# Queueing seven small-constant loads later in the weight stream of a two-layer backbone kernel

## Chip, cores and metric

One Trainium2 chip, one core of it. The metric is the device time of one execution in microseconds (us); for a program on one core that is the time of this core. Several executions are summed up by their median.

## What is computed

The reference is a two-layer block of a flow-matching generator over 512 latent tokens and 256 context tokens of width 1024, in float32. What matters here is its beginning. A conditioning vector for the latent tokens and one for the context tokens go through SiLU and are multiplied by a 1024 x 6144 matrix per layer; that gives six modulation vectors per stream (shift, scale and gate of two sub-layers):

```
s_lat = silu(c);  s_ctx = silu(c_ctx)[None]
mod_l = split((s_lat @ ada_w[layer] + ada_b[layer])[:, None, :], 6)
mod_c = split((s_ctx @ ada_w[layer] + ada_b[layer])[:, None, :], 6)
a_lat = rms_norm(h, ln1_g) * (1 + mod_l[1]) + mod_l[0]
a_ctx = rms_norm(hc, ln1_g) * (1 + mod_c[1]) + mod_c[0]
```

Layer 0 then multiplies both by a combined input projection (the columns of a gated DeltaNet part and of a grouped-query attention part), and uses some small constants: two vectors of 16 (`dt_bias`, `a_log`) for the gates, norm gains of 64 for the output, the queries and the keys (`go`, `gq`, `gk`), a table of cosines and sines for the rotary embedding (`rope`), short convolution weights (`cw`) and two triangular masks for the cumulated gates. After the mixer comes a routed mixture of 16 experts; layer 1 is a neighbourhood attention and again a mixture of experts, and a final norm ends it.

## The kernel before, in words

All large weights pass through a ring of eight slots of 512 KB in SBUF (`RING = 8`). A list named `stream` fixes their order: first the 32 modulation units of layer 0 (kind "ada", units 0 to 31: rows of 128 of `ada_w`, 1024 columns each, for shift and scale), then twelve units of the input projection (kind "blk": four `wrest` of 288 KB, four `wq` and four `wz` of 512 KB), then modulation units 32 to 47 of layer 0 (the gates), all 48 modulation units of layer 1, the convolution part of the projection, and so on. The function `stream_units` (L2286 and on) walks this list on the SP engine. Before unit u it waits until unit u - 8 has been used (`w_free`), and then issues the one DMA of the unit (L2294 for "ada", L2312 for "blk").

Ahead of the stream SP issues five loads (L2322 to L2326): identity and ones (`base`), the conditioning vectors (`cT`), the norm gains (`lnT`), the selection matrix (`sel`) and the modulation bias (`adab`). Behind the fifth modulation unit, inside `stream_units`, it issues the tokens: `ctx` (1 MB, L2296) and `x` (2 MB, L2297) into the tile H. Right behind these come the small constants of later stages: `masks` (L2299), `dt_bias`, `a_log` and `go` (one loop, L2302), `gq` (L2303), `gk` (L2305), `rope` (L2307) and `cw` (L2308). These eight loads write 128, 8, 8, 32, 256, 64, 128 and 18 KB, 642 KB or 0.65 MB together. Seven of these are counted by one semaphore, `masks` by its own. `dt_bias`, `a_log`, `go`, `gq` and `gk` are read with a stride of zero over the 128 partitions; `gq` is also repeated eight times and `gk` twice within a partition, so that these two are written in runs of 64 values (256 bytes), 1024 runs and 256 runs. SP issues in program order, so every later unit stands behind them.

TensorE takes the 32 modulation units one by one (`ada_matmuls`, its matmuls at L241), each as soon as it has landed, and each frees its slot. Then VectorE adds the bias (L274), TensorE transposes the vectors into columns (L249), VectorE copies and combines them (L284, L291) and normalises the six token tiles (L342), TensorE transposes these (`norm_pe`, L366) while VectorE and ScalarE apply scale and shift (L353, L330), and TensorE begins the input projection (`proj_pe`, L458), whose first group of eight matmuls needs all four `wrest` units. ScalarE squares the tokens for their norm (L318) when `ctx` and `x` have landed.

The first users of the small constants: VectorE at L498 (in `gates_dve`, which waits for all seven with `qtp_load` before it), TensorE at L536 for the masks (in `gates_pe`), and after these the head norms with their gains and the rotary table, the convolution and the output norm.

Of the kernel before, what the change touches and what calls it, by code (L numbers as in the profile page):

```python
# [141 lines left out]
def build(nc, t, out):  # L142

    ctx = ExitStack()
    with ctx:
# [81 lines left out]
        def ada_unit(l, n):  # L227

            r, k, i = n // 16, n % 16 // 2, n // 16 + 3 * (n % 2)
            return t["ada_w"][l, k * P:(k + 1) * P, i * D:(i + 1) * D], r, k, i  # L230
# [2055 lines left out]
        def stream_units(sp, lo, hi):  # L2286
            for u in range(lo, hi):
                kind, args = stream[u]
                if u >= RING:
                    sp.wait_ge(w_free, u - RING + 1)  # L2290
                slot, sig = ring[:, u % RING, :], w_land[u % RING]
                if kind == "ada":
                    l, n = args
                    sp.dma_start(slot, ada_unit(l, n)[0]).then_inc(sig, 16)  # L2294
                    if (l, n) == (0, 4):
                        sp.dma_start(H[:, 0:CT, :], t["ctx"].rearrange("(t p) d -> p t d", p=P)).then_inc(x_in, 16)  # L2296
                        sp.dma_start(H[:, CT:NT, :], t["x"].rearrange("(t p) d -> p t d", p=P)).then_inc(x_in, 16)  # L2297
                    if (l, n) == (0, 4):
                        sp.dma_start(MSUM, t["masks"].rearrange("p (d n) -> p d n", d=2)) \  # L2299
                            .then_inc(masks0_in, 16)  # L2300
                        for dst, name in ((DTB, "dt_bias"), (ALOG, "a_log"), (GO, "go")):
                            sp.dma_start(dst, t[name].partition_broadcast(P)).then_inc(qtp_load, 16)  # L2302
                        sp.dma_start(GAIN[:, 0:512].rearrange("p (h d) -> p h d", d=HD),  # L2303
                                     t["gq"].partition_broadcast(P).unsqueeze(1).broadcast_to([P, 8, HD])).then_inc(qtp_load, 16)
                        sp.dma_start(GAIN[:, 512:640].rearrange("p (h d) -> p h d", d=HD),  # L2305
                                     t["gk"].partition_broadcast(P).unsqueeze(1).broadcast_to([P, 2, HD])).then_inc(qtp_load, 16)
                        sp.dma_start(ROPE, t["rope"].rearrange("p (t w c) -> p t w c", t=LT, w=2)).then_inc(qtp_load, 16)  # L2307
                        sp.dma_start(CW, t["cw"].rearrange("p (c w) -> p c w", w=3)).then_inc(qtp_load, 16)  # L2308
                elif kind == "blk":
                    b, k2 = args  # L2310
                    N = 2 * WIDTH[b]
                    sp.dma_start(slot[:, 0:N], t[("wrest", "wq", "wz")[b]][k2]).then_inc(sig, 16)  # L2312
                elif kind == "conv":
                    sp.dma_start(slot, t["wconv"][args[0]]).then_inc(sig, 16)
                elif kind in ("wout0", "wout1", "wv"):
                    sp.dma_start(slot, t[kind][args[0] * P:(args[0] + 1) * P, :]).then_inc(sig, 16)
                else:
                    sp.dma_start(slot, t[kind][args[0]]).then_inc(sig, 16)

        @block.sync  # L2320
        def _(sp):
            sp.dma_start(base_t[:, :], t["base"]).then_inc(consts_in, 16)  # L2322
            sp.dma_start(cT, t["cT"]).then_inc(small_in, 16)
            sp.dma_start(lnT_t[:, :], t["lnT"]).then_inc(small_in, 16)
            sp.dma_start(SEL, t["sel"].rearrange("p (s m) -> p s m", s=8)).then_inc(consts_in, 16)
            sp.dma_start(rows_t[:, :], t["adab"][0]).then_inc(rows_in, 16)  # L2326
            stream_units(sp, 0, U_OUT0)
            dn_sync(sp)
            stream_units(sp, U_OUT0, U_MOE[0])
            rows_sync(sp, 0)  # L2330
            moe_sync(sp, 0)
            sp.wait_ge(mp["x_free"], 24 * NPAIR)
            stream_units(sp, U_MOE[0], len(stream))
            rows_sync(sp, 1)
            moe_sync(sp, 1)
            for i in range(LT):
                sp.wait_ge(end_ok, i + 1)
                sp.dma_start(out[i * P:(i + 1) * P, :], FIN[:, i, :]).then_inc(all_out, 16)
            sp.wait_ge(all_out, 16 * LT)
# [136 lines left out]
```

## Time and profile before

| | |
|---|---|
| median of 3 runs | 2627.17 us (2625.91 to 2636.28) |
| the profiled execution, own time | 2635.99 us |
| its span in the trace | 2634.2 us |
| mean granted TensorE clock | 0.914 of full |
| TensorE matmul busy | 2160.6 us (82%) |
| VectorE, ScalarE, GpSimd busy | 697.3, 462.5, 171.6 us |
| chain that ended last | PE 63%, DMA 22%, DVE 10%, ACT 2% |

The page cuts the span into 40 equal slices of 65.9 us. The row of PE gives its busy share in tenths, PEclk the granted clock in tenths, DMA the mean busy share of the 16 DMA engines; here the first slices matter, of which the first has PE at 4, DMA at 8 and the second PE at 8, DMA at 2. The chain of work that ended last is followed back from the last instruction: what stands in it set the end of the program, and what does not stand in it was covered by something else. In the trace an issue (SPq) is the time that SP's queue spends on a DMA instruction; when the data has landed is told separately, as a time from the issue on.

### The profile page before, as it was taken

The page shows a single profiled execution, that of the slowest core. Times are in us where ns is not written, and L with a number is a line of the kernel's source. Part 1 is how long each engine was busy: PE and PEld are TensorE (multiplying, and loading weights), DVE is VectorE, ACT ScalarE, POOL GpSimd, SP SyncE. Part 2 cuts the span into 40 slices and gives each one's busy share as a digit, 9 for nine tenths or more (in the row PEclk, how much of TensorE's full clock was granted, in tenths as well). Part 3 has the DMA queues.
Part 4 walks back from the last instruction along what each step waited for, and adds up shares of the span by engine and source line. Part 5 has one row for each costly group of instructions (what it writes and reads, how often), then busy time and mean ns, then how long its engine had stood idle before and what let it go on. Part 6 is the DMA issues. An engine that isn't in the chain of part 4 may idle for free.

```text
span 2634.2 us, 31425 instructions
## 1 busy us (share of the span) xinstructions
PE 2160.6 (82%) x13016; PEld 1117.4 (42%) x13016; DVE 697.3 (26%) x1289; ACT 462.5 (18%) x1025; POOL 171.6 (7%) x156
## 2 busy tenths in 40 slices
PE   4897999963786957999999977999999487777774
PEld 0543566643686433333333323554895222222221
DVE  0205332259867251001111112000553500000001
ACT  1014322166520011000000002000551100000001
POOL 0000000011111000111111010000000000000000
PEclk8898999985757988999999988999999699999997
DMA  8215532014112337999999971111212399999996
GB/s 308 109 41 206 159 120 81 15 34 129 65 34 97 136 137 265 369 388 385 394 393 393 399 265 40 56 32 62 83 49 89 128 387 413 415 414 415 414 415 236
DMA packets 113955, 564.30 MB, mean 214 GB/s; under 512 B 13552, under 2 KB 26352, under 8 KB 64672
## 3 DMA queue, kind: packets, MB, share of 16 engines
q1 hardware_dynamic: 102080, 522.55, 50.9%
q0 software_dynamic: 10416, 34.58, 4.8%
q10 hardware_dynamic: 1328, 5.24, 0.6%
q8 instruction: 104, 1.70, 0.3%
q14 instruction: 27, 0.22, 0.0%
HBM read 532.87 MB, written 29.46 MB: 213 GB/s over the span
## 4 chain that ended last, share of the span: by engine, by line
PE 63%; DMA 22%; DVE 10%; ACT 2%; issue 2%; SPq 1%; POOL 0%; DVEq 0%; ACTq 0%; POOLq 0%
PE ps L1805 14%; DMA work_sb<-expert_w_up 8%; PE ps L1569 5%; PE ps L1813 5%; DMA work_sb<-expert_w_gate 5%; DMA work_sb<-expert_w_down 5%; PE ps L458 4%; PE ps L2071 4%; PE ps L754 3%; PE ps L643 2%; PE ps L2049 2%; PE ps L2058 2%; PE ps L241 2%; PE ps L2134 2%; DMA ring_sb<-ada_w 2%
## 5 line engine op out<-in xcount | busy, mean ns | idle before, releaser
L1805 PE MATMUL ps<-work_sb 128*32 128x512 f32 (+1 forms) x2304 | 364.9, 600 | 75.3 <-DMA work_sb<-expert_w_gate 32.3
L1805 PE MATMUL ps<-ring_sb,work_sb 128*32 128x512 f32 (+1 forms) x2304 | 362.6, 601 | 64.2 <-DMA ring_sb<-expert_w_up 27.9
L1805 PEld LDWEIGHTS ps<-work_sb 128*32 128x32 f32 (+1 forms) x2304 | 114.3, 120 | 308.4 <-issue 308.0
L1805 PEld LDWEIGHTS ps<-ring_sb,work_sb 128*32 128x32 f32 (+1 forms) x2304 | 108.6, 120 | 290.2 <-issue 272.3
L1913 DVE TENSOR_TENSOR work_sb<-ps,work_sb 128x512 f32<-128x512 f32 x32 | 20.6, 686 | 658.5 <-PE ps L1813 330.4
L1569 PE MATMUL ps<-ring_sb,work_sb 128*128 128x512 f32 x320 | 139.6, 599 | 2.7 <-DVE work_sb L2199 1.9
L241 PE MATMUL ps<-ring_sb,sT_sb 128*32 128x512 f32 x384 | 99.3, 674 | 42.1 <-DMA ring_sb<-ada_w 42.1
L1884 ACT ACTIVATE work_sb<-ps 128x1024 f32<-128x1024 f32 x16 | 16.4, 1024 | 606.9 <-PE ps L1805 306.5
L1964 POOL DMA_INDIRECT hl_rows<-work_sb x32 | 45.6, 1426 | 966.1 <-DVE work_sb L1927 868.3
L458 PE MATMUL ps<-ring_sb,work_sb 128*128 128x512 f32 (+1 forms) x288 | 105.9, 530 | 0.9 <-DVE work_sb L353 0.9
L1813 PE MATMUL ps<-ring_sb,work_sb 128*32 128x512 f32 x768 | 101.1, 596 | 0.0
L1813 PE MATMUL ps<-work_sb 128*32 128x512 f32 x768 | 100.7, 592 | 0.0
L754 PE MATMUL ps<-work_sb,ring_sb 128*128 128x512 f32 x192 | 98.0, 592 | 0.0
L2071 PE MATMUL ps<-ring_sb,work_sb 128*128 128x512 f32 x224 | 96.3, 592 | 0.0
L1569 PEld LDWEIGHTS ps<-ring_sb,work_sb 128*128 128x128 f32 x320 | 61.2, 192 | 79.8 <-issue 76.2
L1927 DVE SCALAR_TENSOR_TENSOR work_sb<-ps,work_sb,gates_sb 128x1024 f32<-128x1024 f32 x16 | 20.6, 1284 | 281.5 <-PE ps L1813 149.8
L1889 ACT COPY work_sb<-ps 128x512 f32<-128x512 f32 x32 | 17.9, 588 | 349.2 <-PE ps L1852 349.1
L458 PEld LDWEIGHTS ps<-ring_sb,work_sb 128*128 128x128 f32 x288 | 54.6, 190 | 51.6 <-issue 45.4
L643 PEld LDWEIGHTS ps<-work_sb 128*128 128x128 f32 x448 | 53.5, 191 | 39.4 <-issue 38.6
L2058 PE MATMUL ps<-work_sb,ring_sb 128*128 128x512 f32 x128 | 65.3, 592 | 0.0
L2071 PEld LDWEIGHTS ps<-ring_sb,work_sb 128*128 128x128 f32 x224 | 42.6, 190 | 53.6 <-issue 53.6
L695 DVE TENSOR_REDUCE work_sb<-ps 128x1 f32<-128x768 f32 (+1 forms) x48 | 37.4, 780 | 102.9 <-PE ps L633 80.9
(363 smaller groups left out, 2805.5 us busy)
## 6 DMA issues: line engine op xcount, KB each, us to landing
work_sb<-expert_w_gate SPq DMA_DIRECT2D x64, 1024.0 KB, 9.6
ring_sb<-expert_w_gate SPq DMA_DIRECT2D x64, 1024.0 KB, 13.3
ring_sb<-expert_w_up SPq DMA_DIRECT2D x64, 1024.0 KB, 16.2
work_sb<-expert_w_up SPq DMA_DIRECT2D x64, 1024.0 KB, 14.0
ring_sb<-expert_w_down SPq DMA_DIRECT2D x64, 1024.0 KB, 15.4
work_sb<-expert_w_down SPq DMA_DIRECT2D x64, 1024.0 KB, 12.9
ring_sb<-ada_w SPq DMA_DIRECT2D x96, 512.0 KB, 5.0
ring_sb<-wout SPq DMA_DIRECT2D x16, 512.0 KB, 6.4
```

The source lines that it names most:

```text
L241: mm = pe.matmul(ps[32 * q:32 * q + 32, bank, :], sT[:, k, :], w[:, a * 512:(a + 1) * 512], start=(k == 0), stop=(k == KT - 1))
L458: mm = pe.matmul(ps[:, j % 4, 0:N], A[:, k, tok_cols(tt):tok_cols(tt) + P], w[:, (k % 2) * N:(k % 2 + 1) * N], start=(k == 0), stop=(k == ...
L643: mm = pe.matmul(ps[:, 6, n % 8 * HD:(n % 8 + 1) * HD], PT[:, n % 2, c * P:(c + 1) * P], VB[:, c, kv * HD:(kv + 1) * HD], start=(c == 0), ...
L754: mm = pe.matmul(ps[:, b, :], w[:, k, :], A[:, k, LO:LO + LAT], start=(k == 0), stop=(k == KT - 1))
L1569: mm = pe.matmul(ps[:, 4 + j % 4, :], c(k), w[:, half * 512:half * 512 + 512], start=(k == 0), stop=(k == KT - 1))
L1805: mm = pe.matmul(ps[g:g + wide, bank + n, :], lat_src[:, k, g:g + wide], us[e][:, n * 512:(n + 1) * 512], start=(k == 0), stop=(k == KT - 1))
L1813: mm = pe.matmul(ps[g:g + 32, bank_c, :], ctx_src(k, e), us[e][:, n * 512:(n + 1) * 512], start=(k == 0), stop=(k == KT - 1))
L1964: pool.indirect_dma_start(hl_rows, at(TOKH[0:CAP_L, 2 * p + e:2 * p + e + 1]), YL0[r], None, compute_op=ALU.add) \
L2049: mm = pe.matmul(ps[:, c % 4, :], w[:, k, :], AO[:, k, LO:LO + LAT], start=(k == 0), stop=(k == KT - 1))
L2058: mm = pe.matmul(ps[:, b, :], w[:, k, :], AO[:, k, LO:LO + LAT], start=(k == 0), stop=(k == KT - 1))
L2071: mm = pe.matmul(ps[:, 2 * (m % 2) + half, :], AO[:, k, v_cols(m):v_cols(m) + P], w[:, half * 512:half * 512 + 512], start=(k == 0), stop= ...
L2134: mm = pe.matmul(ps[:, 5 + g % 2, n % 8 * HD:(n % 8 + 1) * HD], OPT[:, n % 2, c * P:(c + 1) * P], VO[:, m, h * HD:(h + 1) * HD], start=(c ...
```

## The change

The condition under which the small constants are issued names modulation unit 31 in place of unit 4. The two token loads, `ctx` and `x`, stay behind unit 4. Nothing else differs: the same eight loads, in the same order, with the same semaphores, now behind the 32nd unit and ahead of the first `wrest` unit.

```diff
@@ -2295,7 +2295,7 @@
                     if (l, n) == (0, 4):
                         sp.dma_start(H[:, 0:CT, :], t["ctx"].rearrange("(t p) d -> p t d", p=P)).then_inc(x_in, 16)
                         sp.dma_start(H[:, CT:NT, :], t["x"].rearrange("(t p) d -> p t d", p=P)).then_inc(x_in, 16)
-                    if (l, n) == (0, 4):
+                    if (l, n) == (0, 31):
                         sp.dma_start(MSUM, t["masks"].rearrange("p (d n) -> p d n", d=2)) \
                             .then_inc(masks0_in, 16)
                         for dst, name in ((DTB, "dt_bias"), (ALOG, "a_log"), (GO, "go")):
```

## Rows read from the trace of the kernel before

**Rows 1.** The chain that ended last, 0 to 260 us: start us, us, what.

```profile
12.91 6.80 SPq L2305
...
22.38 17.18 DMA ring_sb<-ada_w
39.60 4.50 PE ps L241 x12
...
93.30 105.96 PE ps L458 x288
```

**Rows 2.** Six stretches: us, PE, PEld, DVE, ACT, POOL busy, PEclk, DMA share, GB/s.

```profile
15.70:22.00 6.30, 0.04 (x2) 0.00 (x0) 0.00 (x0) 0.00 (x0) 0.00 (x0) 0.85 1.03 401
22.00:32.00 10.00, 0.00 (x0) 0.00 (x0) 0.00 (x0) 7.92 (x14) 0.00 (x0) 0.50 0.09 23
32.00:39.60 7.60, 0.00 (x1) 0.00 (x1) 0.00 (x0) 0.00 (x0) 0.00 (x0) 0.50 0.66 249
39.60:74.20 34.60, 28.86 (x104) 4.05 (x104) 0.69 (x1) 0.00 (x0) 0.00 (x0) 0.89 1.01 396
...
93.30:199.00 105.70, 105.70 (x288) 54.63 (x288) 3.77 (x19) 7.78 (x12) 5.22 (x1) 1.00 0.15 49
```

**Rows 3.** Timeline of SP's DMA issues, 0 to 260 us: start us, us, engine line.

```profile
6.80 2.10 SPq L2299 DMA_DIRECT2D work_sb<-masks  x1
...
12.43 0.44 SPq L2303 DMA_DIRECT2D work_sb<-gq  x1
...
21.90 0.43 SPq L2308 DMA_DIRECT2D work_sb<-cw  x1
22.38 41.63 SPq L2294 DMA_DIRECT2D ring_sb<-ada_w  x27
64.95 6.54 SPq L2312 DMA_DIRECT2D ring_sb<-wrest  x4
```

**Rows 4.** DMA packets of the stretch 24 to 28 us.

```profile
DMA packets 256, 0.07 MB, mean 16 GB/s; under 512 B 256, under 2 KB 256, under 8 KB 256
```

**Rows 5.** DMA issues, 0 to 260 us: KB each, median us from issue to landing.

```profile
ring_sb<-wrest SPq DMA_DIRECT2D x4, 288.0 KB, 7.9
...
work_sb<-gq SPq DMA_DIRECT2D x1, 256.0 KB, 21.7
...
work_sb<-gk SPq DMA_DIRECT2D x1, 64.0 KB, 22.7
...
work_sb<-cw SPq DMA_DIRECT2D x1, 18.0 KB, 16.5
```

**Rows 6.** Timeline of all engines, 0 to 130 us: start us, us, engine line.

```profile
14.69 1.05 PE L241 MATMUL ps<-ring_sb,sT_sb 128*32 128x512 f32 x4 [0.23 <-DMA ring_sb<-ada_w]
...
22.32 1.06 ACT L318 ACTIVATE work_sb<-h_sb 128x1024 f32<-128x1024 f32 x1 [18.51 <-DMA h_sb<-x]
...
39.60 6.14 PE L241 MATMUL ps<-ring_sb,sT_sb 128*32 128x512 f32 x20 [23.86 <-DMA ring_sb<-ada_w]
...
61.30 1.05 PE L241 MATMUL ps<-ring_sb,sT_sb 128*32 128x512 f32 x4 [0.22 <-DMA ring_sb<-ada_w]
...
62.58 1.05 PE L241 MATMUL ps<-ring_sb,sT_sb 128*32 128x512 f32 x4 [0.23 <-DMA ring_sb<-ada_w]
...
66.64 1.05 PE L241 MATMUL ps<-ring_sb,sT_sb 128*32 128x512 f32 x4 [1.73 <-DMA ring_sb<-ada_w]
...
74.22 1.05 PE L241 MATMUL ps<-ring_sb,sT_sb 128*32 128x512 f32 x4 [0.20 <-DMA ring_sb<-ada_w]
...
97.48 0.29 DVE L484 COPY work_sb<-ps 128x128 f32<-128x128 f32 x1 [4.24 <-PE ps L458]
...
117.50 0.26 DVE L498 TENSOR_TENSOR work_sb<-work_sb 128x96 f32<-128x96 f32 x1
```

**Rows 7.** Matmuls with the masks (L536): count, duration ns, first and last start us.

```profile
L536 PE MATMUL ps<-work_sb x24: 269/361/363, 204.2 to 211.1; 128*128 128x8 f32 x24
```

**Rows 8.** SP's waits over the whole span: us in total, times, longest us.

```profile
SPq L1979 <- PE ps L1813: 475.7, 92, 57.9
```

## The prediction
> **What bounds the kernel now.** I read the chain that ended last first, and in it only the start, since the change touches nothing behind the input projection by itself. There the chain goes through SP's issue of `gk`, then through the wait of modulation unit 5 for its data, then through the modulation matmuls, and at 93.30 us it enters 106 us of gap-free projection matmuls [rows 1]. So the time to the first L458 matmul lies on the path in full. The timeline tells how it is spent [rows 6]: units 0 to 4 are used by 15.74 us; unit 5 starts at 39.60, after 23.86 us without a matmul; then a unit starts every 1.28 us (61.30, 62.58), with one hiccup ahead of 66.64; the last, unit 31, starts at 74.22; 19.08 us later the projection starts.
>
> Next the stretches [rows 2]. Up to 22.0 us the 16 DMA engines are full (share 1.03, 401 GB/s): that part of the hole is `ctx` and `x`, and ScalarE gets `x` at 22.32 [rows 6]. From 22 to 32 us the share is 0.09 at 23 GB/s, and the stretch 24 to 28 us moves 256 packets, all below 512 bytes [rows 4]: 64 a us. That is the pattern of `gq`'s 1024 runs of 256 bytes, issued at 12.43 [rows 3] and landed 21.7 us later [rows 5], at 34.1. `gk` lands at 12.91 + 22.7 = 35.6 and `cw` at 21.90 + 16.5 = 38.4, and unit 5, issued at 22.38, starts at 39.60, right behind them. So the queue is worked off in order, and small runs hold up the large load behind them. During the modulation stream itself the bound is the DMA (396 GB/s; a unit is 1.05 us of matmul in a beat of 1.28).
>
> **The change part by part.**
>
> Removed from behind unit 4: eight loads, 0.65 MB, and 22.33 - 6.80 = 15.5 us of SP's issue time [rows 3]. Units 5 to 7 then follow `x` at 6.75 us. The DMA engines are full until 22.0 and would simply go on: unit 5 is there one beat after `x`, at 22.32 + 1.28 = 23.6, against 39.60. That is 16.0 us. Some bytes of the constants moved before 22 us beside `x`: of the 0.65 MB, 0.23 moved from 22 to 32 us (10 us at 23 GB/s) and the 0.15 of `rope` and `cw` later, which leaves 0.27 MB, 0.7 us at 401 GB/s. The gain is between 16.0 and 16.7 us; I take 16.5, unit 5 at 23.1.
>
> Kept: the beat. 26 units from 39.60 to 74.22 take 34.62 us, hiccup and all. TensorE's clock was at 0.50 in the rows from 22 us on [rows 2], the lower level of 1.2 GHz, and even so the first five units took 6.14 us [rows 6], 1.23 each, below the beat. The idle time left, 15.7 to 23.1 us, still lets the clock fall (0.85 as the mean of 15.7 to 22.0), so those first units run slow again, hidden behind the DMA. I cost the clock at nothing; with the cover gone it would be (1.23 - 1.05) x 5 = 0.9 us. Unit 31 starts at 74.22 - 16.5 = 57.7 us, and the projection is ready for its weights at 93.30 - 16.5 = 76.8.
>
> Added behind unit 31: the same eight loads, ahead of `wrest`, `wq` and `wz`. Two resources are passed. (a) SP's queue: unit 31 waits for unit 23's slot, so SP issues it at about 64.0 - 16.5 = 47.5, the constants follow until 47.5 + 15.5 = 63.0 at the old pace, and `wrest` 0 goes out at 63.0. It went out at 64.95 before [rows 3], with 28.35 us in hand against 93.30 and 7.9 us needed [rows 5]: that slack of 20 us pays for the move. (b) The DMA queue: before, a large load became usable 39.60 - 22.32 = 17.3 us after the last large one ahead of the constants. Put behind unit 31 this gives 57.7 + 17.3 = 75.0 for `wrest` 0, against a need at 76.8: cover 1.8 us. The other three are smaller than a modulation unit (288 against 512 KB, 0.7 us a piece) and the eight matmuls of the first group last 4.24 us [rows 6], so they keep ahead. The lower bound: with fewer runs outstanding than at 12.43 us, `gq` may be worked on from its issue, 47.5 + 5.6 = 53.1; its visible work of 34.1 - 22.3 = 11.8 us and the remaining 39.60 - 34.1 = 5.5 us then end at 70.4. The upper bound: unit 5's full 17.2 us from issue to use, counted from 63.0, is 80.2, which is 3.4 us late. I take 75.0, since it measures the queue from the last large landing, which is how the rows line up; so nothing is lost, and both ends are kept for the range. A late `wrest` would delay TensorE one for one; `wq`, issued next, has 23 us more.
>
> Users of the constants: they have landed by about 75 us. The first user, L498, would run at 117.50 - 16.5 = 101.0 [rows 6], and the masks are first read at 204.2 - 16.5 = 187.7 [rows 7]. Cover 26 us and more: no cost. No wait is added on any engine, and `qtp_load`, on which VectorE and ScalarE wait, is complete long before.
>
> Behind 93.30: TensorE is busy for all of 105.70 us at full clock [rows 2]. Further on SP's issues wait for slots that matmuls free, the largest such wait being 475.7 us in the expert stage [rows 8]; SP thus cannot run ahead on its own, and all that follows should move as a block.
>
> Sum: 16.5 us gained, nothing given back. On the profiled execution: 2635.99 - 16.5 = 2619.5 us. That execution is 8.8 us above the median of 2627.17, so the same difference there gives **2610.7 us**, 0.63% less.
>
> A page weighed against the rows: the stretch 22 to 32 us shows small runs at 23 GB/s. The Trainium skill, DMA: Bandwidth & Descriptors, section "Anatomy of one DMA", fits a transfer as 2.0 us plus its bytes at 436 GB/s (measured for loads issued from GpSimd). By that fit the constants' 0.65 MB would occupy the engines for 1.5 us, and the sum would be about 1.5 us instead of 16.5. The trace disagrees with it for this queue. The same page, section "Bandwidth", says that transfers under 64 KB are descriptor-dominated; with that the rows agree.
>
> **The rivals.**
>
> *Late weights.* The hole moves from unit 5 to the first `wrest` instead of vanishing. For it: the cover is only 1.8 us, and by issue time it is -3.4. Against it: fewer loads are outstanding when `gq` is issued, 4.6 us of stream (57.7 - 53.1) against 9.9 (22.3 - 12.4). Price: up to 3.4 us, plus perhaps 1 us for a TensorE whose clock is lower; the gain is then 12.1 to 16, at worst 2627.17 - 12.1 = 2615.1 us.
>
> *Slower than before.* The constants are worked off one load at a time: place, the DMA queue between unit 31 and `wrest`. If `gk` began only when `gq` had landed, both with their full times, then 53.1 + 21.7 + 22.7 + (39.60 - 35.6) = 101.5, 24.7 us past the need of 76.8; less the 16.5 gained that is 8.2 us slower, 2635.4, and over 0.5% slower from 29.6 us of lateness on. It decides from a landing of `wrest` 0 after 93.3. Against it: before, `gk` landed 1.5 us after `gq`, and 64 packets a us would have to become half as many.
>
> *The bytes alone matter.* The hole from 22 to 39 us isn't the constants' but follows on any load behind `x`; removing them gives their 0.65 MB, 0.65 / 0.401 = 1.6 us, and the time is 2625.6. Against it: that stretch holds nothing but small packets. The Trainium skill's fit, quoted above, would come out there too.
>
> That the change does not do what it says is hardly possible: unit (0, 31) is in the list once, and ahead of `wrest`.
>
> **How the numbers follow.** A measurement of this kernel can tell about 0.5% (13.1 us) from no change; the three runs shown already spread by 10.4 us. Forecast 0.76, late weights 0.16, bytes alone 0.05, slower 0.03. The forecast's 16.5 clears the 13.1 by 3.4 us, and scatter of medians eats that in about 1 of 6 cases: 0.64 faster, 0.12 same. Late weights: 0.07 faster, 0.09 same. Bytes alone: same. The slow rival: 0.02 slower, 0.01 same. Together 0.71, 0.27, 0.02. The range takes the gain from 12.1 to 16.7 and about 4 us of scatter on either side, rounded: 2606 to 2619, with a little more on the low side since the highest of the three runs shows that the scatter of before is not centred: 2605 to 2619.
>
> **What would show each step.** Right: no idle time of TensorE over 9 us before 60 us; unit 5 at 22.5 to 24 us; DMA share near 1 up to 57 us, and only then a stretch of about 0.06 to 0.1; unit 31's matmul at 57 to 58.5; first L458 at 76 to 78 with VectorE as its releaser. Wrong: that matmul released by the DMA of `wrest`, a first L458 past 80, a hole left at unit 5, or a projection longer than 106 us. If all these fit and the time is still not 16 us lower, something behind 93 us did not move with the block, and the forecast is wrong there.

## The result, and the profile after

Twenty runs of the changed kernel have a median of 2617.38 us (2609.35 to 2627.28), twenty of the kernel before 2628.98 us (2623.09 to 2636.42). The ratio is 0.995 with a 95% interval of 0.9941 to 0.9959: 0.5% faster, about 13.1 us, between 10.8 and 15.5. (The two medians alone differ by 11.6 us, 0.44%.) The profiled execution took 2622.86 us with a span of 2621.1 us (mean granted clock 0.917). The forecast was 2610.7 us, 0.63% less; the time lies inside the range of 2605 to 2619, and the gain is 3 to 5 us smaller than the 16.5 forecast.

The chain that ended last, first 260 us of the changed kernel, answers to [rows 1] (start us, us, what). SP's issues of `gk` have left it, the wait of unit 5 ends at 23.3 instead of 39.6, and the projection enters at 77.07 instead of 93.30 with the same 105.96 us of work:

```profile
6.62 16.68 DMA ring_sb<-ada_w
23.35 4.52 PE ps L241 x12
...
77.07 105.96 PE ps L458 x288
```

The timeline of all engines, which answers to [rows 6]:

```profile
22.04 1.06 ACT L318 ACTIVATE work_sb<-h_sb 128x1024 f32<-128x1024 f32 x1 [17.86 <-DMA h_sb<-x]
...
23.35 6.19 PE L241 MATMUL ps<-ring_sb,sT_sb 128*32 128x512 f32 x20 [7.95 <-DMA ring_sb<-ada_w]
...
50.28 1.05 PE L241 MATMUL ps<-ring_sb,sT_sb 128*32 128x512 f32 x4 [1.55 <-DMA ring_sb<-ada_w]
...
57.96 1.05 PE L241 MATMUL ps<-ring_sb,sT_sb 128*32 128x512 f32 x4 [0.22 <-DMA ring_sb<-ada_w]
...
77.07 53.16 PE L458 MATMUL ps<-ring_sb,work_sb 128*128 128x288 f32 x165 [0.91 <-DVE work_sb L353]
...
101.27 0.26 DVE L498 TENSOR_TENSOR work_sb<-work_sb 128x96 f32<-128x96 f32 x1
```

Unit 5 starts one beat after `x`; TensorE's idle time before it fell from 23.86 to 7.95 us. The hiccup in the stream is there again (1.55 us, at 50.28). The first projection matmul is still released by VectorE, not by a DMA, so the weights were there.

SP's issues, which answer to [rows 3], and below them the time to landing of `gq` and `gk`, which answers to [rows 5]:

```profile
6.62 41.21 SPq L2294 DMA_DIRECT2D ring_sb<-ada_w  x27
47.87 1.00 SPq L2299 DMA_DIRECT2D work_sb<-masks  x1
...
50.33 0.43 SPq L2303 DMA_DIRECT2D work_sb<-gq  x1
50.81 4.36 SPq L2305 DMA_DIRECT2D work_sb<-gk  x1
...
58.35 10.01 SPq L2312 DMA_DIRECT2D ring_sb<-wrest  x4
```

```profile
work_sb<-gq SPq DMA_DIRECT2D x1, 256.0 KB, 16.2
...
work_sb<-gk SPq DMA_DIRECT2D x1, 64.0 KB, 17.7
```

The slow stretch of the DMA has moved, it has not vanished. Stretches of the changed kernel (columns as in [rows 2]):

```profile
23.00:58.00 35.00, 29.00 (x106) 4.05 (x108) 0.69 (x1) 6.97 (x14) 0.00 (x0) 0.88 0.99 390
...
58.00:60.00 2.00, 1.12 (x5) 0.24 (x6) 0.69 (x1) 0.00 (x0) 0.00 (x0) 1.00 0.07 18
60.00:62.00 2.00, 1.10 (x8) 0.90 (x8) 0.87 (x13) 0.00 (x0) 0.00 (x0) 1.00 0.07 20
...
68.00:70.00 2.00, 2.00 (x11) 1.90 (x10) 0.92 (x2) 0.67 (x2) 0.00 (x0) 0.50 0.68 174
70.00:72.00 2.00, 2.00 (x12) 1.97 (x10) 1.51 (x2) 1.02 (x2) 0.00 (x0) 0.50 0.99 320
```

It now lies under the bias add, the transposes and the normalisation, which wait for no weights, and is over by 70 us, before the projection asks for them.

### The profile page after: what moved, and what is told of

The parts are those of the page before. It is cut to its first block, busy times and chain, and to the rows that moved or that the text cites. A ratio compares the mean times of both kernels' runs of the same rounds, so it can differ in the third digit from the quotient of the medians.

```text
span 2621.1 us, 31425 instructions
## 1 busy us (share of the span) xinstructions
PE 2159.6 (82%) x13016; PEld 1113.8 (42%) x13016; DVE 698.7 (27%) x1289; ACT 462.1 (18%) x1025; POOL 169.9 (6%) x156
## 4 chain that ended last, share of the span: by engine, by line
PE 63%; DMA 22%; DVE 9%; ACT 2%; issue 2%; SPq 1%; POOL 0%; DVEq 0%; ACTq 0%; POOLq 0%
PE ps L1805 14%; DMA work_sb<-expert_w_up 7%; PE ps L1569 5%; PE ps L1813 5%; DMA work_sb<-expert_w_gate 5%; DMA work_sb<-expert_w_down 5%; PE ps L458 4%; PE ps L2071 4%; PE ps L754 3%; PE ps L643 2%; PE ps L2049 2%; PE ps L2058 2%; PE ps L241 2%; PE ps L2134 2%; DMA ring_sb<-expert_w_up 2%
## 5 line engine op out<-in xcount | busy, mean ns | idle before, releaser
L1805 PE MATMUL ps<-work_sb 128*32 128x512 f32 (+1 forms) x2304 | 364.9, 600 | 74.2 <-DMA work_sb<-expert_w_gate 32.7
L1805 PE MATMUL ps<-ring_sb,work_sb 128*32 128x512 f32 (+1 forms) x2304 | 365.0, 605 | 66.5 <-DMA ring_sb<-expert_w_up 31.0
L1805 PEld LDWEIGHTS ps<-work_sb 128*32 128x32 f32 (+1 forms) x2304 | 114.5, 120 | 306.9 <-issue 306.5
L1805 PEld LDWEIGHTS ps<-ring_sb,work_sb 128*32 128x32 f32 (+1 forms) x2304 | 109.4, 121 | 293.7 <-issue 275.9
L1569 PE MATMUL ps<-ring_sb,work_sb 128*128 128x512 f32 x320 | 139.6, 599 | 2.7 <-DVE work_sb L2199 1.9
L458 PE MATMUL ps<-ring_sb,work_sb 128*128 128x512 f32 (+1 forms) x288 | 105.9, 530 | 0.9 <-DVE work_sb L353 0.9
L1813 PE MATMUL ps<-ring_sb,work_sb 128*32 128x512 f32 x768 | 101.4, 598 | 0.0
L1813 PE MATMUL ps<-work_sb 128*32 128x512 f32 x768 | 100.7, 592 | 0.0
L1927 DVE SCALAR_TENSOR_TENSOR work_sb<-ps,work_sb,gates_sb 128x1024 f32<-128x1024 f32 x16 | 20.5, 1284 | 280.5 <-PE ps L1813 149.8
L1569 PEld LDWEIGHTS ps<-ring_sb,work_sb 128*128 128x128 f32 x320 | 61.2, 192 | 79.8 <-issue 76.2
L458 PEld LDWEIGHTS ps<-ring_sb,work_sb 128*128 128x128 f32 x288 | 54.6, 190 | 51.6 <-issue 45.4
## 6 DMA issues: line engine op xcount, KB each, us to landing
ring_sb<-expert_w_down SPq DMA_DIRECT2D x64, 1024.0 KB, 13.6
work_sb<-expert_w_down SPq DMA_DIRECT2D x64, 1024.0 KB, 12.7
```

The lines of the kernel that those rows point to most:

```text
L458: mm = pe.matmul(ps[:, j % 4, 0:N], A[:, k, tok_cols(tt):tok_cols(tt) + P], w[:, (k % 2) * N:(k % 2 + 1) * N], start=(k == 0), stop=(k == ...
L1569: mm = pe.matmul(ps[:, 4 + j % 4, :], c(k), w[:, half * 512:half * 512 + 512], start=(k == 0), stop=(k == KT - 1))
L1805: mm = pe.matmul(ps[g:g + wide, bank + n, :], lat_src[:, k, g:g + wide], us[e][:, n * 512:(n + 1) * 512], start=(k == 0), stop=(k == KT - 1))
L1813: mm = pe.matmul(ps[g:g + 32, bank_c, :], ctx_src(k, e), us[e][:, n * 512:(n + 1) * 512], start=(k == 0), stop=(k == KT - 1))
```

## The experiments

Twelve runs were made, eight of variants and four of unaltered copies. The comparisons with the kernel before use its runs on the same chip. A ratio is the time over that of the kernel before, with its 95% interval. "L458" below is the start of the first projection matmul, 93.30 us in the profile of before and 77.07 in that of the changed kernel.

### Which load makes the hole: e1 and e2

The first moves `gq` alone behind unit 31, the second moves the other seven and leaves `gq`. The edit of e1, shortened:

```diff
-                        sp.dma_start(GAIN[:, 0:512]..., t["gq"]...)          # at (0, 4)
...
+                    if (l, n) == (0, 31):
+                        sp.dma_start(GAIN[:, 0:512]..., t["gq"]...)
```

> Only the load of gq (1024 runs of 256 bytes) is moved behind unit 31; the other seven constants stay behind unit 4. Theory 'runs' (the hole is made by the number of small runs, most of them gq's): gq's visible 11.8 us go, unit 5 starts at about 27.8 us instead of 39.60, and the first L458 matmul at about 81.5. Rival 'any load behind x' (the small loads hold up the stream by being there, not by their runs): seven of eight loads remain, so unit 5 stays past 36 us and L458 past 90.

> gq alone stays behind unit 4, the other seven constants go behind unit 31. Theory 'runs': gq keeps its 11.8 us and only the rest of the hole goes; unit 5 at about 35 us, first L458 at about 89. Rival 'any load behind x': one of eight loads remains, unit 5 at 25 us or earlier, L458 at 79.

With `gq` alone late, unit 5 starts at 29.58 us and L458 at 82.70, a gain of 10.6 us in the profile; the ratio is 0.9963 (0.9949 to 0.9978). With `gq` alone left, unit 5 starts at 35.13 and L458 at 88.57, a gain of 4.7; the ratio is 0.9983 (0.9964 to 1.0001). Both are within 2 us of what was expected for `gq` as the main part, and unit 5 is over 6 us from where "any load behind x" wanted it. The two parts add up to 15.3 of the 16.2 us.

### Number of runs or their source: e3, e4 and e8

e3 keeps the order and lays the repeats into the row, so that `gq` is 128 runs of 2 KB (and `gk` 128 runs of 512 bytes). e4 keeps `gq`'s 1024 runs of 256 bytes, but gives each an address of its own. The edit of e4, shortened:

```diff
-        gq=c(a["even_q_norm_g"][0]),
+        gq=c(np.tile(a["even_q_norm_g"][0], (P, 8, 2))),
...
-                                     t["gq"].partition_broadcast(P).unsqueeze(1).broadcast_to([P, 8, HD]))
+                                     t["gq"][:, :, 0:HD])
```

> All eight constants stay behind unit 4, but gq and gk come from inputs laid out with the repeats inside the row, so that gq is 128 runs of 2 KB and gk 128 runs of 512 bytes: the same 320 KB are written, in 256 runs instead of 1280. Theory 'runs': 1024 runs fewer, unit 5 at 26 to 29 us, first L458 at 80 to 83. Rival 'bytes alone': the same bytes, so unit 5 stays at 39.6 and L458 at 93.3.

> All constants stay behind unit 4; gq is again written in 1024 runs of 256 bytes, but every run is read from an address of its own, 512 bytes from the next, instead of all from the same 256 bytes. Theory 'runs': nothing changes, unit 5 at 38.5 to 40.5 us. Rival 'one source' (reading the same 256 bytes 1024 times is what is slow): the hole shrinks as with wide rows, unit 5 at 26 to 29 us.

e3: unit 5 at 28.35 us, L458 at 82.11, ratio 0.9966 (0.9948 to 0.9985). So the bytes are not it. But e3 alone can't tell the number of runs from the number of reads of one address, since it lowers both.

e4 can, and it refutes the reading that I had put on record, that small runs as such are slow: with as many runs of the same size, unit 5 starts at 28.36 us and L458 at 81.23; ratio 0.9957 (0.9935 to 0.9979). `gq` lands 11.4 us after its issue at 12.58, at 24.0, instead of at 34.1. The timeline of TensorE in e4:

```profile
28.36 4.91 PE L241 MATMUL ps<-ring_sb,sT_sb 128*32 128x512 f32 x16 [12.49 <-DMA ring_sb<-ada_w]
```

DMA packets of e4 in the stretch 20 to 24 us, and of the kernel before in the same stretch:

```profile
DMA packets 2089, 1.14 MB, mean 285 GB/s; under 512 B 1748, under 2 KB 1949, under 8 KB 2089
```

```profile
DMA packets 1036, 0.83 MB, mean 207 GB/s; under 512 B 769, under 2 KB 897, under 8 KB 1036
```

1748 small packets in 4 us are 437 a us, those of all loads together; before, 769 passed in the same stretch (192 a us), and behind it 64 a us [rows 4]. So what makes the greater part of the hole is that the 1024 reads go to the same 256 bytes. Why such reads are slow no run shows, and no distance but 512 bytes was tried.

e8 reads all five broadcast constants from addresses of their own, again with the order of before:

> The kernel before with its order (all constants behind unit 4), but all five broadcast constants (dt_bias, a_log, go, gq, gk) read every run from an address of its own, in the same number of runs. Theory 'one source': what is left of the hole is the bytes and a little for the number of runs, so unit 5 starts at 25 to 27 us (28.36 with gq alone apart) and the first L458 at 78 to 80, nearly what the move gives. Rival 'runs': unit 5 stays at 28 us or later, because the number of runs is as before.

Its unit 5 starts at 26.59 us, inside the 25 to 27 expected, and L458 at 80.28, 0.3 us past the 80; ratio 0.9953 (0.9937 to 0.9968). All eight constants stay ahead of unit 5 and the hole is nearly gone. What is left against the changed kernel, 26.59 - 23.35 = 3.2 us, is by my estimate 1.6 us of bytes (0.65 MB at 401 GB/s) and 1.6 us that I leave to the number of runs without having tested it.

### A queue of their own: f2

The kernel before, with the eight loads issued by ScalarE's queue at about 4 us (`act.dma_start` behind the first activation), so that the stream isn't behind them.

> The kernel before, but the eight constants are issued by ScalarE, right after its first activation (about 4 us), so that they have a queue of their own and the weight stream doesn't stand behind them. Theory 'one queue' (the slow reads of one row hold up only what is queued behind them on the same queue): the DMA engines stay full, unit 5 starts at 24 to 26 us, first L458 at 77.5 to 79.5. Rival 'the engines are held' (the slow reads keep the DMA engines themselves from other work): a hole of some 10 us stays wherever they run, unit 5 or a later unit is late, and L458 starts past 85.

Unit 5 starts at 35.12 us and L458 at 89.51; ratio 0.9993 (0.9974 to 1.0011). The theory "one queue" falls. The first L458 comes 3.8 us earlier than before, not 16, and the ratio can't be told from no change. The stream is not queued behind the constants and is held up all the same: `x` lands later (ScalarE's first square at 31.12 instead of 22.32). Stretches of that kernel (columns as in [rows 2]):

```profile
18.00:22.00 4.00, 0.00 (x0) 0.00 (x0) 0.00 (x0) 0.00 (x0) 0.00 (x0) 0.72 0.79 213
22.00:26.00 4.00, 0.00 (x0) 0.00 (x0) 0.00 (x0) 0.00 (x0) 0.00 (x0) 0.50 0.85 233
26.00:30.00 4.00, 0.00 (x0) 0.00 (x0) 0.00 (x0) 0.00 (x0) 0.00 (x0) 0.50 0.64 209
34.00:38.00 4.00, 2.88 (x8) 0.38 (x8) 0.00 (x0) 3.98 (x9) 0.00 (x0) 0.50 1.00 383
```

From 22 to 26 us 211 small packets pass, 53 a us, much as in [rows 4]; large packets pass beside them, and all together the engines move little more than half of what they moved before. The packets of that stretch by queue, SP's (q1) and ScalarE's (q10), with MB and share of the engines:

```profile
q1 hardware_dynamic: 214, 0.88, 79.4%
q10 hardware_dynamic: 211, 0.05, 5.7%
```

The two queues get as many packets through as each other, here and in every stretch of 2 us from 12 to 34 us (192 and 190 from 12 to 14, 98 and 98 from 30 to 32). So the engines work the two queues packet for packet, and the large loads are held to the pace of the slow reads. The Trainium skill, DMA: Bandwidth & Descriptors, section "Issuing engines are not separate DMA queues", says that DMAs of all issuing engines run on the same 16 engines and interleave; this run agrees. Where such loads stand in time counts for more than which queue they are on.

### How much cover the move has: e7

The changed kernel, with `gq` issued twice behind unit 31, the second time into a free area (`SQJ`), and the two waits for the constants raised from seven loads to eight.

> The changed kernel with the load of gq issued twice behind unit 31, the second time into a scratch area that is free then. It measures the cover of the first wrest unit. A second gq costs the DMA queue 1024 reads of one 256-byte row, at the 64 a us of the trace 16 us. If the cover is the 1.8 us of the prediction, the first L458 matmul waits for the DMA of wrest and starts at about 77.1 + 14.2 = 91.3; if it is 5 us, as the changed kernel's DMA share suggests (near 1 from 70 us on), at 88; if the weights were there much earlier (10 us or more), at 83 or before.

The timeline of that kernel around its first projection matmul:

```profile
76.89 5.22 POOL L2445 MEMSET work_sb<- 128x6144 f32 x1 [75.83 <-DVE work_sb L353]
86.57 1.46 PEld L458 LDWEIGHTS ps<-ring_sb,work_sb 128*128 128x128 f32 x4 [10.78 <-issue]
86.60 1.78 PE L458 MATMUL ps<-ring_sb,work_sb 128*128 128x288 f32 x3 [10.62 <-DMA ring_sb<-wrest]
```

GpSimd's memset starts when the activations are complete, at 76.89; TensorE starts 9.7 us later, when `wrest` lands. That is between the 83 and the 88 expected, nearest to a cover of 5 us. The rival "late weights" is real as a mechanism. TensorE waits one for one, and after this idle time it starts at the lower clock (0.53 as the mean of 86.6 to 92 us), so that the projection itself takes 108.43 instead of 105.95 us: 2.5 us more, where the prediction had put "perhaps 1 us". `gk` lands at 55.63 + 27.7 = 83.3 us instead of 50.81 + 17.7 = 68.5, so the second `gq` cost the queue 14.8 us. By this estimate `wrest` would have been usable without it at 86.60 - 14.8 = 71.8 us, and the cover in the changed kernel is 77.07 - 71.8 = 5.3 us.

### Something else to move: f1

The changed kernel, and `sel` (512 KB) goes behind unit 31 as well, its wait with it.

> The changed kernel, and the selection matrix sel (512 KB, first read by the gate matmuls past 200 us) goes with the constants behind unit 31 too, ahead of them. If the stretch up to unit 31 is bound by the bytes ahead of it, 0.52 MB at 410 GB/s are 1.3 us: first L458 at 75.8 instead of 77.07, still released by VectorE. Rival 'the cover is used up': wrest now stands behind 0.52 MB more and the first L458 waits for its DMA, at 77 or later.

Half a miss. L458 starts at 76.78 us, released by VectorE, so the cover held; but of the 1.3 us expected only 0.3 came, and unit 5 did not come earlier at all (23.58). Its DMA moved 335 GB/s from 4 to 8 us and 368 from 8 to 12, against 387 and 402 in the changed kernel: what was taken out ahead was given back by a slower start, which I can't explain. The ratio is 0.9944 (0.9923 to 0.9966); no difference to the changed kernel (0.995) can be told from that, and no other variant has a lower ratio than the changed kernel.

### Where the rest of the gain went: e5, e6, f3 and f4

Unaltered copies, to see what one profile is worth.

> The changed kernel once more, unaltered, for a second profile of it. Theory 'scatter' (the 3 us by which the gain at the end of the profiles falls short of the 16.2 us at the projection come from stretches that last differently from one execution to the next: the gate matmuls at L259, the DeltaNet stage, the expert stage of layer 0): the first L458 again at 77 us within 0.5, but at least one of these three stretches differs from the first profile by over 2 us. Rival 'given back by the change': all three stretches last as in the first profile within 1 us.

> The kernel before once more, unaltered, for a second profile. Theory 'scatter': the first L458 at 93.3 us within 0.5, and at least one of the three stretches (L259 to L599, L993 to L1569, L1805 to the last L1813) differs from the first profile of before by over 2 us. Rival 'given back by the change': they repeat within 1 us.

> The changed kernel for a third profile. From the start of L259 to the start of L599 its first two profiles took 14.6 and 13.8 us, against 11.0 and 12.4 in the two of before. Theory 'the clock at L259 depends on where the work falls': 13.5 us or more again. Rival 'chance': anything from 11 to 14.6.

> The kernel before for a third profile, to go with the third of the changed one. Theory 'the clock at L259 depends on where the work falls': at most 12.8 us from L259 to L599 again, and the first L458 at 92.5 to 93.5. Rival 'chance': anything from 11 to 14.6.

Durations of stages in us, and in the first row the start of the first L458; three executions each (before; e6; f4 and after; e5; f3):

| | before | after |
|---|---|---|
| first L458 | 93.3, 92.6, 92.2 | 77.1, 77.0, 76.9 |
| L458 to first L599 | 147.3, 148.4, 147.5 | 150.9, 150.3, 150.7 |
| of it L259 to L599 | 11.0, 12.8, 11.1 | 14.6, 13.8, 16.2 |
| L599 to DeltaNet (L993) | 329.1, 329.1, 329.0 | 329.0, 329.0, 330.7 |
| L993 to L1569 | 293.6, 291.5, 287.2 | 291.6, 287.4, 288.3 |
| experts of layer 0 (L1805 to last L1813) | 544.6, 544.5, 545.5 | 548.3, 544.1, 544.8 |

The first L458 of e6 (92.64) and of f4 (92.23) lie 0.2 and 0.3 us below the ranges expected for them, and the "12.4" in the expectation of f3 is 12.8 in the trace. Two things come out. First, scatter: the DeltaNet stage lasts 287.2 to 293.6 us whichever kernel it is, and the experts 544.1 to 548.3; a single pair of profiles can show from 7.9 us (f4 and after) to 20.5 us of gain (before and e5) at the end of the span. The first theory, that all of the shortfall is of this kind, is not enough, though: the stretch from L458 to L599 does not scatter much and is longer in the changed kernel, 150.6 against 147.8 on average, 2.9 us. It is the gate matmuls (L259). Of the kernel before, then of the changed one, from the timeline of TensorE:

```profile
229.59 1.96 PE L259 MATMUL ps<-modrows_sb,work_sb 128*128 128x512 f32 x4 [1.89 <-DVE modrows_sb L274]
232.65 1.99 PE L259 MATMUL ps<-modrows_sb,work_sb 128*128 128x512 f32 x4 [1.10 <-ACT gates_sb L267]
```

```profile
213.35 3.75 PE L259 MATMUL ps<-modrows_sb,work_sb 128*128 128x512 f32 x4 [2.19 <-DVE modrows_sb L274]
218.21 3.78 PE L259 MATMUL ps<-modrows_sb,work_sb 128*128 128x512 f32 x4 [1.10 <-ACT gates_sb L267]
```

The same four matmuls take 3.75 instead of 1.96 us, twice over. The granted clock says why; two stretches of the kernel before, up to L259 and from there on, then the same two of the changed kernel:

```profile
211.80:227.80 16.00, 12.46 (x55) 2.60 (x55) 13.29 (x22) 6.37 (x11) 0.00 (x0) 0.71 0.66 233
228.00:240.00 12.00, 7.10 (x15) 2.71 (x16) 11.73 (x23) 3.04 (x3) 0.00 (x0) 0.98 0.52 209
```

```profile
195.50:211.50 16.00, 12.45 (x55) 2.64 (x55) 13.23 (x22) 6.36 (x11) 0.00 (x0) 0.71 0.64 232
211.80:221.80 10.00, 7.35 (x8) 2.35 (x8) 9.79 (x20) 1.01 (x1) 0.00 (x0) 0.50 0.61 248
```

In both kernels the clock falls to its lower level (0.50, 1.2 GHz) after TensorE has waited for the last modulation units (2.27 us before, 2.01 after); read in rows of 1 us it stays there for some 3 us in this profile of before, and for some 13 us in that of after, through the first two groups. A slow group by itself is no mark of the changed kernel: in e6, an unaltered copy of before, the first group took 3.75 us too, and in e8 3.36. In the profiles of after, e5 and f3 two or three groups were slow. The stretch from L458 to L599 separates most of the variants: 147.3 to 148.4 us in before, e6, f4, e2, e3, e4, e8 and f2; 150.1 to 151.0 in after, e5, f3, f1 and e1. The second list is kernels that load `gq` behind unit 31, but not all of them. e7 loads it there as well; of its 150.9 us, 2.5 are the slower start of its projection, and the 148.5 that are left put it beside the first list, with a single slow group (3.64 us). From L259 to L599 it is 13.6 to 16.2 us in the second list against 11.0 to 12.8 in the first and 12.7 in e7. I have no cause for it: in the two profiles shown the waits of TensorE ahead of L259 differ by 0.3 us (1.89 and 2.19) and the mean clock of the 16 us before it is the same, 0.71. "The clock at L259 depends on where the work falls" held in its numbers; but e1 runs L259 at 219.0 us and is slow, e3 runs it at 218.5 and is fast, so the place in time alone is not it. That the 2.9 us come from the change, and not from the executions that happened to be profiled, is likely by these counts and not shown.

With it the account closes as far as the scatter lets one see. The starts of L458 differ by 92.7 - 77.0 = 15.7 us on average; less 2.9 us given back at L259 that is 12.8 us, inside the interval of 10.8 to 15.5. The spans of the same six profiles differ by 15.3 us on average, since the later stages together were 2.5 us shorter in the three of after, which is less than the DeltaNet stage alone scatters.

## Why the prediction was right, and what of it was wrong

- **The hole before unit 5.** Forecast 23.1 us between 22.9 and 23.6; measured 23.35. The DMA engines simply went on behind `x`. Right, and the two bounds held it.
- **The beat and the hiccup.** 26 units in 34.62 us; measured 57.96 - 23.35 = 34.61. Unit 31 at 57.7 against 57.96. The clock was indeed down for the first of them (6.19 us for five units) and the DMA hid it.
- **SP's queue.** Constants at 47.5 against 47.87. The term for their issue was mis-sized: 15.5 us forecast, 58.35 - 47.87 = 10.5 measured. What sets this time is not settled. The number of runs is a part of it: with the order of before, e3 took 18.25 - 6.86 = 11.4 us with `gq` in 128 runs, and e4 22.57 - 7.28 = 15.3 with 1024 runs from separate addresses.
- **The cover of `wrest`.** 1.8 us was taken (usable at 75.0), with 70.4 and 80.2 as bounds; e7 puts it at 71.8 and the cover at 5.3. So the lower bound was the nearer, but its argument, that `gq` is worked on from its issue, is not what the trace shows: `gq` was issued at 50.33, and small packets in number begin between 54 and 56 us (182, against 20 in the 2 us before). The rival "late weights" (0.16) did not come about, and e7 shows that it would have with one more load like `gq`.
- **Users of the constants.** L498 at 101.0 forecast, 101.27 measured, not delayed.
- **Why the reads are slow.** "Small runs hold up the large load behind them" was right in its effect and its price (10.6 us for `gq` alone against 11.8), wrong in its reason. It called in the Trainium skill (DMA: Bandwidth & Descriptors, section "Bandwidth": transfers under 64 KB are descriptor-dominated) and said that the rows agree, but `gq` is 256 KB, and e4 shows a load of that size and as many runs without the hole. The rows at hand showed 64 packets a us and 256 bytes each; they could not tell small from same. e4 did.
- **Nothing given back.** This is the step that failed: "all that follows should move as a block", and the clock costed at nothing. The prediction's own last sign says so: all signs up to the projection fit, and the time is not 16 us lower. The clock was checked where it is hidden (the modulation stream) and where TensorE is busy without a break (L458), but not at L259, where TensorE works in bursts between waits; there 2.9 us went. (The argument also misread a row: 475.7 us is the sum of 92 waits of SP, the longest of them 57.9 us [rows 8].)
- **The bytes alone (0.05).** By the constants' bytes at 401 GB/s the hole would have shrunk by 1.6 us; it shrank by 16.25. The Trainium skill's fit (DMA: Bandwidth & Descriptors, section "Anatomy of one DMA") gives an estimate of 1.5 us. It does not describe such a load.
- **The total.** 0.63% forecast, 0.5% measured (0.41 to 0.59). Of the 6.7 us between 2610.7 and 2617.38, 1.8 are the median of before, which came out at 2628.98 with more runs, 0.8 are the start of the projection (15.7 us earlier on average of three profiles each, 16.5 forecast), 2.9 are L259, and the rest is within the interval. The time lies 1.6 us inside the end of the range, and the 4 us allowed for scatter hold it there: the medians' difference of 11.6 us is less than the smallest gain (12.1) that the range was built from. The prediction gave 0.71 to a gain clear of 0.5% (13.1 us). The gain came out at that limit, not clear of it. (It also counted the rival "slower than before" as mostly over that limit, though the price it worked out, 8.2 us, is below it.)

## What to carry to other kernels

When a DMA stretch shows a share of 0.06 with small packets, ask not only how long the runs are but where they come from: a constant broadcast by reading one short row a thousand times cost over ten microseconds here. Laying it out so that each read has an address of its own left 3.2 us of that for all constants (e8), and loading it when no large load is urgent left none, as long as it keeps within the cover (5.3 us here). Moving such loads to another issuing queue gave 3.8 of 16.2 us (f2). A gain at the front of a kernel need not arrive whole at its end: the clock can take some of it where TensorE works in bursts; two profiles are not enough to see which, so set the stages of three or more side by side.

## What the runs showed of the hardware that was not expected

- Reads of 256 bytes from one address ran at 64 a us; with the same 1024 runs read from addresses 512 bytes apart, small packets of all loads passed at 437 a us (e4).
- On a queue of their own these reads held the large loads to their own pace, packet for packet (214 and 211 in 4 us); all together moved at 209 to 233 GB/s instead of some 400 (f2).
- TensorE's clock stayed at its lower level for 10 us instead of recovering, with the same matmuls and a wait longer by 0.3 us. From the projection to L599 that was 2.9 us on average over three profiles of each kernel. It showed in e1 and f1 too, less in e7, and for one group of four matmuls also in e6 and e8, which load `gq` early. The cause stays open.
